# Expert weights of the second half of the tokens: distances to key numbers kept as bytes, one weighting instruction for four tokens, and the result laid by token

## What is computed

```python
idx = jnp.take_along_axis(cidx, pos, axis=-1)        # key0 * 128 + key1
u = jnp.take(peer_u, i_blk, axis=0)
a = jax.nn.gelu(jnp.einsum("td,thkd->thk", x_blk, u)) * g_blk
v = jnp.take(peer_v, i_blk, axis=0)
return jnp.einsum("thk,thkd->td", a, v)
```

## Time and profile before

| | |
|---|---|
| median of three runs | 3110.45 us (3110.15 to 3112.8) |
| span of the profiled execution, first to last instruction | 3108.3 us |
| TensorE busy | 2595.3 us |
| VectorE busy | 2110.1 us |
| ScalarE busy | 1185.0 us |
| GpSimd busy | 800.7 us |
| first weighted row of the second half | at 2558.08 us |
| first slab product | at 2620.47 us |

### The profile page before, as it was taken

How to read it: one execution, slowest core, us unless ns; L and a number is a source line. 1 busy time by engine, 2 the same in 40 slices (tenths; PEclk the granted TensorE clock), 3 DMA queues, 4 the chain that set the end, 5 groups by cost and what they waited for, 6 DMA issues and landing times. The chain is left out here.

```text
span 3108.3 us, 32992 instructions
## 1 busy us (share of the span) xinstructions
PE 2595.3 (83%) x11801; PEld 2024.8 (65%) x11801; DVE 2110.1 (68%) x2948; ACT 1185.0 (38%) x2024; POOL 800.7 (26%) x563
## 2 busy tenths in 40 slices
PE   7998999999999999999999997667344007999993
PEld 6777878888888878888777897667233005444441
DVE  4996465454544565645446569999999988665668
ACT  4466454343434454535554442121199005000000
POOL 0000000010100000000000004666688865544445
PEclk9999999999999999999999999888655559999997
DMA  9543555655555546546334667999999996999998
GB/s 258 170 148 126 186 177 189 192 187 191 188 189 189 189 149 227 187 148 202 136 115 169 204 217 288 415 409 407 377 421 420 420 393 199 409 409 409 409 407 341
DMA packets 294499, 813.45 MB, mean 262 GB/s; under 512 B 33113, under 2 KB 73281, under 8 KB 260320
## 3 DMA queue, kind: packets, MB, share of 16 engines
q1 hardware_dynamic: 220400, 408.87, 39.4%
q0 software_dynamic: 73728, 402.69, 32.3%
q10 hardware_dynamic: 240, 0.18, 0.0%
HBM read 807.48 MB, written 4.19 MB: 261 GB/s over the span
## 5 line engine op out<-in xcount | busy, mean ns | idle before, releaser
L199 DVE TENSOR_TENSOR wl<-ring,wh 128x1024 fp32r<-128x1024 f32 (+2 forms) x616 | 731.5, 1229 | 641.2 <-ACT wh L194 638.7
L194 ACT CAST wh<-ring 128x1024 fp32r<-128x1024 f32 (+2 forms) x616 | 609.5, 1039 | 647.6 <-PE ps L215 586.8
L213 PE MATMUL ps<-wh,th 128*128 128x512 f32 (+1 forms) x1600 | 630.1, 394 | 10.8 <-DVE wl L199 6.0
L1978 POOL DMA_INDIRECT expert_rows<-in_peer_u,index x256 | 478.1, 1867 | 593.9 <-DVE wl L199 427.0
L215 PE MATMUL ps<-wh,tl 128*128 128x512 f32 (+1 forms) x1600 | 621.3, 388 | 0.0
L214 PE MATMUL ps<-wl,th 128*128 128x512 f32 (+1 forms) x1600 | 620.9, 388 | 0.0
L2383 DVE CUSTOM_DVE_ANT_0 junk<-expert_rows,h 128x2048 f32<-128x2048 f32 x227 | 514.0, 2289 | 26.1 <-DMA expert_rows<-in_peer_u,index 24.6
L2422 DVE SCALAR_TENSOR_TENSOR x_and_pieces<-expert_pieces,const,x_and_pieces 128x1024 f32<-128x1024 f32 x256 | 327.8, 1284 | 166.5 <-DMA expert_pieces<-in_peer_v,const 81.4
L2482 PE MATMUL ps<-expert_slabs,by_expert 128*128 128x512 f32 x1024 | 439.7, 592 | 0.7 <-ACT by_expert L2549 0.7
L2482 PEld LDWEIGHTS ps<-expert_slabs,by_expert 128*128 128x128 f32 x1024 | 194.5, 190 | 245.3 <-issue 244.4
L213 PEld LDWEIGHTS ps<-wh,th 128*128 128x128 f32 x1600 | 301.4, 188 | 76.8 <-issue 8.0
(11 more groups left out here) (348 smaller groups left out, 3010.8 us busy)
## 6 DMA issues: line engine op xcount, KB each, us to landing
ring<-in_w_in SPq DMA_DIRECT2D x80, 1024.0 KB, 5.2
ring<-in_w_up SPq DMA_DIRECT2D x64, 1024.0 KB, 5.3
ring<-in_w_down SPq DMA_DIRECT2D x64, 1024.0 KB, 5.1
expert_slabs<-in_peer_v SPq DMA_DIRECT2D x128, 512.0 KB
ring<-in_w_in SPq DMA_DIRECT2D x68, 512.0 KB, 4.9
ring<-in_w_out SPq DMA_DIRECT2D x32, 1024.0 KB, 5.1
ring<-in_w_peer_q SPq DMA_DIRECT2D x16, 1024.0 KB, 5.3
ring<-in_w_ukv SPq DMA_DIRECT2D x8, 1024.0 KB, 5.3
```

What stands on the lines that cost most here:

```text
L194: self.nc.scalar.copy(self.wh[:, i % 2, two, 0:w], self.ring[:, i, two, 0:w]).then_inc(self.high_ready, 1)
L199: self.nc.vector.tensor_tensor(self.wl[:, i % 2, two, 0:w], self.ring[:, i, two, 0:w], self.wh[:, i % 2, two, 0:w].bitcast(F32), ALU.subtr ...
L213: mm(o, hi, wh, start=start and k == 0, stop=False)
L1978: nc.gpsimd.indirect_dma_start(p.rows[:, n % GR, :], None, peer_u, bass.IndirectOffsetOnAxis(ap=p.index[:, n:n + 1], axis=0)).then_inc(p.l ...
```

## The change

The change concerns the second half of the tokens only.

- **Distances ahead of the weights.** ScalarE writes the distance |iota - key| of all 128 tokens and both keys, 256 instructions of 128 elements, as bytes (`measure_distances`). This stands between the copy of the turned keys and the softmax exponential of the second half, which it precedes now.
- **Weighted rows.** VectorE makes four weighted rows by one instruction over 512 elements (`weighted_rows`): is the byte zero, times the weight. In a round it does this twice, and no columns.
- **Columns.** ScalarE makes all columns, four tokens per instruction, from the bytes (`hot_columns`), and does so behind each read-out.
- **Layout.** The products of the second half are stored by token (`by_token`, the 128 key1 of a token side by side). TensorE's stationary operand for the second half is then `by_token[:, :, m]`, 128 numbers that lie 512 bytes apart. The tokens go in the order 112 to 127, 0 to 111, as the bytes lie in the memory that `by_token` fills (each token's bytes are read before its place, or that of others on them, is written).

```diff
-        by_expert = place("by_expert", [P, NH, NKEYS, P], at=-48 * KB)
+        by_expert = place("by_expert", [P, NKEYS, P], at=-48 * KB)
+        by_token = place("by_token", [P, P, NKEYS], at=16 * KB)
+        apart_first = place("apart_first", [P, 32, 2, NKEYS], U8, at=40 * KB)
+        apart_last = place("apart_last", [P, 16, 2, NKEYS], U8, at=48 * KB)
+        apart_rest = place("apart_rest", [P, 80, 2, NKEYS], U8, at=52 * KB)
...
+        def token_of(place_in_order):
+            return (P - 16 + place_in_order) % P
+
+        def apart(t, n, which):
+            z, t = (apart_first, t) if t < 32 else (apart_last, t - 112) if t >= 112 else (apart_rest, t - 32)
+            return z[:, t:t + n, which, :]
+
+        def experts_of(half, m):
+            return by_token[:, :, m] if half else by_expert[:, m, :]
...
-            def rows_by_vector(at):
+            def weighted_rows(at):
                 dve.wait_ge(hot_used, P + at + 4)
-                for n in range(at, at + 4):
-                    nc.vector.tensor_scalar(row_hot[:, n % 8, :], iota, turned_keys[:, 0, n:n + 1],
-                                            turned_w[:, n:n + 1], ALU.is_equal, ALU.mult).then_inc(rows_hot, 1)
-
-            def cols_by_vector(at):
-                dve.wait_ge(hot_used, P + at + 4)
-                nc.vector.tensor_tensor(col_hot[:, at % 8:at % 8 + 4, :], iota.unsqueeze(1).broadcast_to([P, 4, NKEYS]),
-                                        turned_keys[:, 1, at:at + 4].unsqueeze(2).broadcast_to([P, 4, NKEYS]),
-                                        ALU.is_equal).then_inc(cols_hot[at % 8 // 4], 4)
+                t = token_of(at)
+                nc.vector.scalar_tensor_tensor(out=row_hot[:, at % 8:at % 8 + 4, :], in0=apart(t, 4, 0), scalar=0.0,
+                                               in1=turned_w[:, t:t + 4].unsqueeze(2).broadcast_to([P, 4, NKEYS]),
+                                               op0=ALU.is_equal, op1=ALU.mult).then_inc(rows_hot, 4)
...
+            dve.wait_ge(distances_made, 2 * P)
             for r in range(P // 8):
-                rows_by_vector(8 * r)
-                cols_by_vector(8 * r + 4)
-                rows_by_vector(8 * r + 4)
+                weighted_rows(8 * r)
+                weighted_rows(8 * r + 4)
                 if r == 0:
                     dve.wait_ge(sums_in, 16)
                 add_piece(r)
...
-                        end = mm(core.ps[:, 2 * half + q, :], by_expert[:, half, m, :], slabs[:, m % SLOTS, q * 512:(q + 1) * 512],
+                        end = mm(core.ps[:, 2 * half + q, :], experts_of(half, m), slabs[:, m % SLOTS, q * 512:(q + 1) * 512],
                                  start=m == 0, stop=m == NKEYS - 1)
...
+            def measure_distances():
+                for at in range(P):
+                    t = token_of(at)
+                    for w in range(2):
+                        nc.scalar.activation(apart(t, 1, w), iota, ACT.Abs, scale=-1.0,
+                                             bias=turned_keys[:, w, t:t + 1]).then_inc(distances_made, 1)
+
+            def hot_columns(at):
+                act.wait_ge(hot_used, P + at + 4)
+                if at == 0:
+                    act.wait_ge(distances_made, 2 * P)
+                nc.scalar.activation(col_hot[:, at % 8:at % 8 + 4, :], apart(token_of(at), 4, 1), ACT.Relu, scale=-1.0,
+                                     bias=1.0).then_inc(cols_hot[at % 8 // 4], 4)
+
+            def read_tokens(at):
+                act.wait_ge(hot_used, P + at + 12)
+                if at == 0:
+                    act.wait_ge(freed, NH * PICKS + GR)
+                t = token_of(at)
+                nc.scalar.copy(by_token[:, t:t + 4, :],
+                               core.ps[:, 4 + at % 8 // 4, :].rearrange("p (t k) -> p t k", t=4)).then_inc(read, 1)
...
-            exponentiate(1)
             copy_keys(1)
             act.wait_ge(columns, 3)
+            measure_distances()
+            exponentiate(1)
             nc.scalar.activation(core.small[:, 60:61], turned_keys[:, 0, 0:1], ACT.Gelu_apprx_tanh).then_inc(distant, 1)
-            count = 2 * P + 1
-            hot_by_scalar(count + 4, 1, 0, 0, (1,))
+            hot_columns(0)
+            hot_columns(4)
             gelu(1)
             copy_weight(1)
-            act.wait_ge(freed, NH * PICKS + GR)
-            for r in range(P // 8):
-                read_out(r, 1, 0)
-                if r + 1 < P // 8:
-                    hot_by_scalar(count + 4 * (r + 2), 1, 8 * r, 8, (1,))
-                read_out(r, 1, 1)
+            for at in range(0, P, 4):
+                read_tokens(at)
+                if at + 8 < P:
+                    hot_columns(at + 8)
```

More of the change, by code:

```diff
@@ L22 @@
 U32 = mybir.dt.uint32
+U8 = mybir.dt.uint8
 ACT = mybir.ActivationFunctionType
@@ L2250, in peer_stage @@
             "row_quarters_turned", "row_quarters_laid", "rows_dotted")
+        distances_made, = core.new("distances_made")
         cols_hot = core.new("cols_hot_low", "cols_hot_high")
@@ L2526, in _, with hot_by_scalar @@
         def _(act):
-            def hot_by_scalar(count, half, t, at, which):
-                act.wait_ge(hot_used, t + (half * P + at + 4))
-                for w in which:
+            def hot_by_scalar(count, t, at):
+                act.wait_ge(hot_used, t + (at + 4))
+                for w in range(2):
                     for i in range(4):
@@ L2539, in hot_by_scalar @@
                         (rows_one, cols_hot[at % 8 // 4])[w], 4)
-                if 0 in which:
-                    act.wait_ge(rows_one, t + (half * P + at + 4))
-                    for i in range(4):
-                        n = at + i
-                        nc.scalar.activation(row_hot[:, n % 8, :], row_hot[:, n % 8, :], ACT.Copy,
-                                             scale=turned_w[:, bass.ds(t + n, 1)]).then_inc(rows_hot, 1)
-            def read_out(g, half, bank):
-                act.wait_ge(hot_used, g * 8 + (half * P + bank * 4 + 12))
-                nc.scalar.copy(by_expert[:, half, :, bass.ds(g * 8 + bank * 4, 4)],
-                               core.ps[:, 4 + bank, :].rearrange("p (t k) -> p k t", t=4)).then_inc(read, 1)
+                act.wait_ge(rows_one, t + (at + 4))
@@ new lines, in hot_by_scalar, with read_out @@
+                for i in range(4):
+                    n = at + i
+                    nc.scalar.activation(row_hot[:, n % 8, :], row_hot[:, n % 8, :], ACT.Copy,
+                                         scale=turned_w[:, bass.ds(t + n, 1)]).then_inc(rows_hot, 1)
+            def read_out(g, bank):
+                act.wait_ge(hot_used, g * 8 + (bank * 4 + 12))
+                nc.scalar.copy(by_expert[:, :, bass.ds(g * 8 + bank * 4, 4)],
+                               core.ps[:, 4 + bank, :].rearrange("p (t k) -> p k t", t=4)).then_inc(read, 1)
```

9 lines of the change are left out of this document (4 added, 5 removed).

## The result

| | before | changed |
|---|---|---|
| median of 4 runs, us | 3111.41 (3110.15 to 3112.8) | 3084.04 (3083.05 to 3085.17) |
| ratio to before, 95% interval | | 0.9914 [0.9902, 0.9926] |
| span of the profiled execution, us | 3108.3 | 3083.3 |

The kernel became 27.4 us faster by the medians, 25.0 by the profiled spans (the changed kernel's profiled execution took 3085.17 in all, the longest of its four). Of the page, these two lines changed most: who is busy, and the DMA's rate slice by slice.

The account below looks back on a forecast made before the run. VectorE was taken to bound the spread, the DMA what follows. The stage, 4.43 + 15 x 2.6 + 0.8 = 44.2 against 62.4 us, gains 18.2: span 3108.3 - 18.2 = 3090.1, plus 2.15 gives 3092.3 us, range 3087 to 3105.

Parts of the forecast that it names:

- What bounds the kernel: Two stages: VectorE decides in the second half's spread, 3.86 us a round; behind it the DMA does, at 409 GB/s.
- Whatever the spread gives back moves both streams, slabs and pieces, forward by the same amount: Behind the spread: TensorE has 33.6 us of slack, so time saved in the spread moves slabs and pieces forward equally.
- the stage: From first weighted row to first slab product: 62.4 us before, 44.2 forecast, a gain of 18.2 us.
- What follows is fixed work: From the first slab product on, 240 pieces and all slab products are left, in the changed kernel too.
- rival A: In the spread, VectorE's two-tensor instructions lock out GpSimd's gathers; VectorE runs dry, 5 us each time; median 3094 to 3105.
- The round: One spread round of eight tokens: VectorE 2.41 us, loop through TensorE and ScalarE 2.44; 2.44 to 2.75, taken as 2.6.
- slip: In the spread's rounds, something must slip between three almost level engines, part of why 2.6 us was taken.
- The first round: The spread's first round stays at 4.43 us, because its addition waits for a piece that comes no sooner.
- The distances: ScalarE's 256 instructions of 0.32 us, 82 us, between the halves fit in its waits and end near 2498: cost 0.
- The strided loads: TensorE's second-half weight loads grow from 0.19 to 0.30 us, hidden as long as they stay within 0.43 us.
- B: Strided weight loads lengthen the slabs once a load passes 0.53 us; at 0.62 the median is 3157; chance 0.10.
- C: The spread's gain doesn't reach the end because something else binds the pieces: 3110; chance 0.06 with everything else eating the gain.

Follow-up runs that it names:

- E8: The changed kernel with only the last of its 32 row instructions written as four single-tensor ones: 3090.6 us, ratio 0.9935 to the kernel before.
- e2: The kernel before, with VectorE's run of additions behind the spread broken once by a wait for the first slab's products: 3107.12 us, ratio 0.9988.
- e1: The kernel before with only the layout edited, the second half stored by token: 3111.74 us, ratio 1.0001.
- e3: The changed kernel with weighted rows made one by one from floats, as before: 3102.81 us, ratio 0.9976 to the kernel before.
- e4: The changed kernel with columns shared as before, four by VectorE and four by ScalarE: 3103.53 us, ratio 0.9975 to the kernel before.
- e7: The changed kernel with four extra 128 x 512 products on TensorE before the second half's weights come: 3085.98 us, ratio 0.992 to the kernel before.
- e9: The changed kernel with loads of the first six slabs started only after all dots: 3086.86 us, ratio 0.9922 to the kernel before.
- e10: The changed kernel with each of the first six slabs loaded only behind a used piece: 3085.5 us, ratio 0.9917 to the kernel before.
- e5: The changed kernel with no additions in the spread's rounds, all 256 behind it: 3104.22 us, ratio 0.9979 to the kernel before.

## Why the prediction was wrong, point by point

**What bounds the kernel: right for the kernel before.** VectorE in the spread, the DMA behind it, at 409 GB/s in both kernels. In the changed spread the loop through the others is as long as VectorE's work, as the prediction's bounds said.

**"Whatever the spread gives back moves both streams, slabs and pieces, forward by the same amount": the step that failed.** The prediction put the gain at the stage's 18.2 us and nothing else ("What follows is fixed work"). The streams behind it shrank from 472.1 to 466.4 us, by 5.8. The earlier trace rows showed the price in before: a gather of 8.92 us, then VectorE 5.02 us without a piece. The forecast read that row only as a danger that the changed rounds might catch (rival A), and not as a cost that stood in before and could go with the instructions ahead of it. E8 puts it back by four instructions (streams +5.8), e2 takes most of it out of before (median -4.0), and over all kernels it goes with the form of the last rows: with single-tensor rows the gather takes 8.91 or 8.92 (before, e1, e3, e8; 2.93 with the pause of e2), with the new form 1.73 or 1.74 (changed, e4 to e7, e9, e10).

**The round: 2.6 taken, 2.43 measured; a mis-sized term.** The bounds were 2.44 to 2.75, and the round came out at the lower one. VectorE's sum was 2.41 and the loop's 2.44 by rows; e5 measures the loop at 2.42. What was added on top, slip and up to 0.3 us a round for the gather, did not come. The 0.3 was no cost in the kernel before either; it is a misreading of the earlier trace rows. The four rows beside the gather start at 2608.79 and the columns behind them at 2609.83, 1.04 us later; the four others start at 2610.43, and the next instruction is this one:

```profile
2611.45 1.27 DVE L2422 SCALAR_TENSOR_TENSOR x_and_pieces<-expert_pieces,const,x_and_pieces 128x1024 f32<-128x1024 f32 x1
```

That is 1.02 us. One of the rows beside the gather is shown as longer (0.548 against 0.336 us), and this is where the chain's 1.33 comes from; but the next instruction starts 0.256 us behind it as always, and the chain's link for the columns is shorter for it (0.39 where other rounds have 0.60). So the gather costs a round 0.02 us in the old form, and 0.03 in the new one: two row instructions take 1.31 us with a gather's start (2595.32 and the gather at 2595.67), 1.28 to 1.29 without. 15 rounds x 0.17 = 2.6 us.

**The first round: right in its length, the reason only in part.** 4.37 us from 2559.38 to the next row (4.43 taken). VectorE's only wait in it is for the piece:

```profile
2559.38 1.29 DVE L2371 SCALAR_TENSOR_TENSOR row_hot<-apart_last,turned_weight 128x512 f32<-128x512 uint8 x2 [1.02 <-ACT turned_weight L2600]
2562.55 1.28 DVE L2433 SCALAR_TENSOR_TENSOR x_and_pieces<-expert_pieces,const,x_and_pieces 128x1024 f32<-128x1024 f32 x1 [1.88 <-DMA expert_pieces<-in_peer_v,const]
```

But the chain that ended last runs through TensorE there, which the prediction left out:

```profile
2560.17 3.77 PE ps L2486 x16
2563.96 0.59 ACT by_token L2581
2564.55 1.59 PE ps L2486 x12
```

TensorE had been idle, its granted clock is 0.50 (1.2 GHz) from 2558 to 2564, and its first sixteen matmuls, one round, take 3.75 us, where those of a later round take 2.14 at 1.00 (2.4 GHz). It starts its second round at 2564.53, and the rows for it are ready at 2564.44 (2563.75 + 0.69), so both paths end within 0.1 us of each other. No run had the piece sooner or the clock full, and what the first round would be then is not shown. Moving the slabs doesn't shorten it (e9, e10). The stage: 4.37 + 15 x 2.43 + 1.2 = 42.0, against 44.2 forecast (the 1.2, from the last round's end at 2600.17 to 2601.36, was taken at 0.8).

**The distances: right.** ScalarE's timeline between the halves, against the 80.01 and 57.04 of the earlier trace rows:

```profile
2416.43 9.46 ACT L2566 ACTIVATE apart_last<-const,turned_keys 128x128 uint8<-128x128 f32 x32
...
2444.48 46.82 ACT L2566 ACTIVATE apart_rest<-const,turned_keys 128x128 uint8<-128x128 f32 x160
2496.67 0.31 ACT L2587 ACTIVATE top<-top 128x128 f32<-128x128 f32 x1 [4.07 <-DVE top L2355]
2557.72 0.31 ACT L2592 ACTIVATE const<-const 128x128 f32<-128x128 f32 x1 [58.19 <-DVE const L2394]
```

256 instructions end at 2491.3, 75 us after the first, 0.293 each (0.32 taken, from 1.28 / 4, which counts the last one's whole length), and ScalarE still waits 4.07 us for the maximum. They cost nothing.

**The strided loads: right.** 295 ns (0.30 taken), and the products of both halves stand alike (duration in ns, min/median/max):

```profile
L2493 PE MATMUL ps<-expert_slabs,by_expert x512: 592/592/697, 2601.4 to 3038.8; 128*128 128x512 f32 x171
...
L2493 PEld LDWEIGHTS ps<-expert_slabs,by_token x512: 291/295/299, 2602.8 to 3040.1; 128*128 128x128 f32 x171
L2493 PE MATMUL ps<-expert_slabs,by_token x512: 592/592/593, 2603.2 to 3040.5; 128*128 128x512 f32 x171
```

The Trainium skill ("SBUF — State Buffer", section "Door 1: The DMA port swizzle") says that an access which goes to a new line each time pays, and gives no size; here the load takes 295 / 190 = 1.55 times as long, in e1 as well, so the trace agrees. It is hidden below the 0.43 us from product to product.

**The rivals.** *A* did not come: no gather in the rounds took more than 1.61 us (1.14 to 1.15 in the last nine), and VectorE never ran dry behind the first round, though all its instructions read two tensors. The Trainium skill ("SBUF — State Buffer", section "SBUF: two separate sides") says that such an operation and a GpSimd operation that reads SBUF exclude each other for a whole instruction. The traces don't agree with it for a gather's issue: issues of 0.94 us pass beside unbroken additions of 1.28, and the 8.92 us span seven of them. Whether an issue counts as such a read is not shown. *B* needed a load of 0.53 us, and it is 0.295. *C*: the last piece is added at 3067.7, 24.9 us sooner, as the DMA's rate said.

**The forecast with both terms mended:** the stage 2.2 us shorter and the 5.8 of the dry spell, 3092.3 - 2.2 - 5.8 = 3084.3. That this is within 0.3 us of the median is partly luck: the four executions alone spread over 2.1 us.

**What stays open:** why single-tensor rows directly ahead of the additions leave a gather locked out until VectorE pauses. The runs show when it happens and what ends it, not the mechanism. Open, too, is what the first round would take with TensorE's clock full. No kernel tried beat the changed one by the median.

## What to carry to other kernels

A stall that stands in the trace near the edited code is a term of the sum, with both signs: ask not only whether the edit will spread it, but whether it takes it away, and what the instructions directly ahead of it are. Where two edits shorten two loops that bind together, each alone can be worth little (8.9 and 1.1 us here) and both together twice their sum (20.4). And a surcharge is read from start to start: an instruction that the trace shows as longer costs nothing if the next one starts as early as ever.

## What the runs showed of the hardware

- The issue of a gather on GpSimd that starts in an unbroken run of VectorE's additions took 8.91 to 8.92 us, until the run of eight ended, if fp32 instructions of one tensor stood directly ahead of the run (before, e1, e3, e8). Behind instructions of two tensors it took 1.73 to 1.74 us, and the next ones 0.94. A pause of VectorE ended it after 2.93 us (e2).
- A single-tensor row instruction on VectorE during which a gather's issue ended took 548 ns instead of 336 (before, 2609.57; the issue ended at 2610.08), but the next one started 0.256 us behind it, as without a gather. A pair of the new form lost 0.03 us, and the gather took 1.15 us instead of 0.94.
- TensorE's granted clock was 0.50 (1.2 GHz) from 2558 to 2562 in before and from 2558 to 2564 in the changed kernel, behind idle time, and sixteen matmuls took 3.75 us there against 2.14 at 1.00 (2.4 GHz). In e7, where four products ended at 2557.07, it was 1.00 from 2558 to 2562 and 0.50 from 2562 to 2564.
- A weight load of 128 x 128 fp32 with a step of 512 bytes took 295 ns, a contiguous one 190.
- The new instruction of two tensors over 512 elements took 684 ns from floats and 684 to 690 from bytes.
- ScalarE's 128 x 128 distances written as bytes follow each other at 0.293 us; written as floats, they do so too (2611.18, 2611.49, 2611.78 and 2612.07 in before), and 1.28 is the time of four from the first start to the last end.
